# Recurrence of a chunked delta rule: the output values of all four chunks behind the last state, and the gram matrices in two groups of two chunks

## What is computed

```python
def step(S, inp):                      # reference, once per token
    r_t, w_t, k_t, v_t, a_t, b_t = inp
    sa = jnp.einsum('bhij,bhj->bhi', S, a_t)
    S = S * w_t[:, :, None, :] + sa[..., None] * b_t[:, :, None, :] + v_t[..., None] * k_t[:, :, None, :]
    y_t = jnp.einsum('bhij,bhj->bhi', S, r_t)
    return S, y_t
```

## Time and profile before

| | |
|---|---|
| median of 3 runs | 1474.78 us (1473.46 to 1477.78) |
| span of the profiled execution | 1471.8 us |
| PE, matmuls | 1432.0 us busy, 97% |
| DVE | 691.5 us busy, 47% |
| ACT | 514.4 us busy, 35% |
| POOL | 579.4 us busy, 39% |
| granted clock of PE | 9 tenths or more of full speed in all 40 slices |

### The profile page before, as it was taken

The page is one execution under the profiler, slowest core; times in us unless marked ns, Lnnn a source line. Parts: engine busy times, 40 slices in busy tenths (PEclk is TensorE's granted clock), DMA queues, the critical chain, the costliest instruction groups (busy, mean ns, idle before and its releaser), DMA issues.

```text
span 1471.8 us, 34271 instructions
## 1 busy us (share of the span) xinstructions
PE 1432.0 (97%) x14670; PEld 1344.3 (91%) x14670; DVE 691.5 (47%) x1447; ACT 514.4 (35%) x856; POOL 579.4 (39%) x740
## 2 busy tenths in 40 slices
PE   4999999999999999999999999999999999899998
PEld 4998999999999899999999999989999899699998
DVE  7117475664847557475664435343353444500000
ACT  6233242422514233242422544434444343322221
POOL 6353241422424134241422434434344443954442
PEclk9999999999999999999999999999999999999999
DMA  5333131311313113131311853735537375345361
GB/s 198 84 91 89 35 94 37 82 53 45 89 38 84 44 45 104 26 98 38 83 52 38 204 134 90 166 94 144 129 95 166 93 170 127 131 130 158 102 165 45
DMA packets 252084, 143.08 MB, mean 97 GB/s; under 512 B 12109, under 2 KB 245006, under 8 KB 251406
## 3 DMA queue, kind: packets, MB, share of 16 engines
q1 hardware_dynamic: 228316, 125.90, 33.6%
q10 hardware_dynamic: 23618, 15.00, 3.5%
HBM read 125.36 MB, written 15.45 MB: 96 GB/s over the span
## 4 chain that ended last, share of the span: by engine, by line
PE 85%; DVE 4%; POOL 3%; ACT 1%; issue 1%; ACTq 0%; DVEq 0%; POOLq 0%
PE acc L483 57%; PE head_banks L929 3%; PE head_banks L934 3%; PE head_banks L919 2%; PE head_banks L871 2%; PE head_banks L1077 1%; PE head_banks L1097 1%; POOL XL L764 1%; PE head_banks L997 1%; PE head_banks L1090 1%; PE head_banks L1046 1%; PE head_banks L986 1%; PE head_banks L838 1%; PE head_banks L967 1%; PE head_banks L886 1%
## 5 line engine op out<-in xcount | busy, mean ns | idle before, releaser
L466 POOL TENSOR_TENSOR WL<-WR,WH 128x256 fp32r<-128x256 f32 (+1 forms) x656 | 507.1, 804 | 858.9 <-ACT WH L456 838.5
L483 PE MATMUL acc<-XH,WH 128*128 128x260 f32 (+1 forms) x2624 | 569.4, 298 | 9.5 <-POOL WL L466 6.9
L483 PE MATMUL acc<-XH,WL 128*128 128x260 f32 (+1 forms) x2624 | 528.5, 283 | 0.0
L483 PE MATMUL acc<-XL,WH 128*128 128x260 f32 (+1 forms) x2624 | 527.7, 283 | 0.0
L483 PEld LDWEIGHTS acc<-XH,WH 128*128 128x128 f32 (+1 forms) x2624 | 404.6, 188 | 39.9 <-issue 28.7
L483 PEld LDWEIGHTS acc<-XL,WH 128*128 128x128 f32 (+1 forms) x2624 | 404.3, 188 | 0.0
L483 PEld LDWEIGHTS acc<-XH,WL 128*128 128x128 f32 (+1 forms) x2624 | 403.7, 188 | 0.0
L456 ACT ACTIVATE WH<-WR 128x1024 fp32r<-128x1024 f32 (+1 forms) x164 | 171.5, 1048 | 121.9 <-PE acc L483 114.6
L491 ACT ACTIVATE AREN<-acc 128x520 f32<-128x520 f32 (+1 forms) x82 | 49.4, 603 | 362.1 <-PE acc L483 354.8
L1929 DVE TENSOR_TENSOR AREN<-head_banks,AREN 128x512 f32<-128x512 f32 x16 | 11.1, 692 | 169.1 <-PE head_banks L1148 169.1
L1723 DVE TENSOR_TENSOR AREN<-AREN,head_banks 128x128 f32<-128x128 f32 x160 | 46.3, 289 | 33.3 <-PE head_banks L929 19.0
(11 more groups left out here) (238 smaller groups left out, 1597.5 us busy)
## 6 DMA issues: line engine op xcount, KB each, us to landing
WR<-in_w_in SPq DMA_DIRECT2D x128, 512.0 KB, 4.1
WR<-in_w_out SPq DMA_DIRECT2D x32, 512.0 KB, 6.9
out<-AREN ACTq DMA_DIRECT2D x32, 256.0 KB, 3.2
AREN<-in_cache_k_win SPq DMA_DIRECT2D x16, 384.0 KB, 8.0
AREN<-in_cache_v_win SPq DMA_DIRECT2D x16, 384.0 KB, 8.9
mix_scratch<-AREN ACTq DMA_DIRECT2D x16, 260.0 KB, 4.2
AREN<-in_x_prompt SPq DMA_DIRECT2D x4, 1024.0 KB, 7.6
AREN<-in_cache_k_win SPq DMA_DIRECT2D x8, 512.0 KB, 6.9
```

The costliest lines, as they stand in the source:

```text
L466: rest = pool.tensor_tensor(WL[:, place, j:j + 2, 0:M], WR[:, k % 4, j:j + 2, 0:M], WH[:, place, j:j + 2, 0:M].bitcast(F32), ALU.subtract)
L483: mm = pe.matmul(acc[0:M, hf, 0:HT], w[:, (4 * g + k) % 3, j, 0:M], x[:, kt, hf * HT:(hf + 1) * HT], start=(kt == 0 and n == 0), stop=(kt ...
```

## The change

The output values of all four chunks are computed in one run behind the last state (`values`), instead of each behind the `rhs` of the next chunk, and signal one step instead of four. In chunks 1 to 3 one projection unit follows `rhs`, and three instead of four follow `s` in chunks 0 to 2. Of the grams, chunks 0 and 1 stand in one group as before, now followed by 3 units; chunks 2 and 3 stand in one group behind `nn01`, with no unit in between and with other banks; `tokb`, `tokk`, `tokv` and `nn23` change their banks, and wait for the masks g20, g21, g30 and g31 in this order (before: `tokk` for g30, `tokv` for g31); 3 units instead of 4 follow `nn23`. The sum of units stays 64. ACT and POOL follow with their feeds: the rounding at unit 49 moves from behind `u2` to behind `rhs3`.

```diff
--- before.py
+++ after.py
@@ -161,12 +161,12 @@
 LV = range(1, LEVELS)
-GRAMS = ("g00", "g01", "g10", "g11", "g20", "g21", "nn01", "g30", "g31")
+GRAMS = ("g00", "g01", "g10", "g11", "nn01", "g20", "g21", "g30", "g31")
 UNITS = 4 * KT
-BEHIND_A = {"lora": 4, "kk": 3, "tail": 5, "bonus": 4, "vec": 4, "g11": 1, "g21": 1, "tokb": 2, "nn23": 4, "dx2b": 2, "dx4b": 2,
+BEHIND_A = {"lora": 4, "kk": 3, "tail": 5, "bonus": 4, "vec": 4, "g11": 3, "tokb": 2, "nn23": 3, "dx2b": 2, "dx4b": 2,
             "qt6b": 1, "dx6b": 1,
-            "rhs0": 1, **{f"u{c}": 1 for c in range(NC)}, **{f"s{c}": 4 for c in range(NC - 1)}, f"s{NC - 1}": 1,
-            f"y{NC - 1}": 2, "st": 2, "mean": 3}
+            **{f"rhs{c}": 1 for c in range(NC)}, **{f"u{c}": 1 for c in range(NC)}, **{f"s{c}": 3 for c in range(NC - 1)},
+            f"s{NC - 1}": 1, "values": 2, "st": 2, "mean": 3}
 QB = T // 128
 JS = [(h, b) for b in range(QB) for h in range(2)]
 BEHIND_B = {"ssum": 6, "tokv": 2, "stok": 2, "qb": 13,
@@ -383,8 +383,7 @@
                       *[x for l in LV if l < last
                         for x in (f"qt{l}a", f"qt{l}b", f"dy{l}a", f"dx{l}a", f"dy{l}b", f"dx{l}b")],
                       *[f"{s}{last}{h}" for s in ("qt", "dx") for h in "ab"],
-                      *[x for c in range(NC) for x in (f"rhs{c}", *([f"y{c - 1}"] if c else []), f"u{c}", f"s{c}")],
-                      f"y{NC - 1}", "st", "mean", "var"])
+                      *[f"{s}{c}" for c in range(NC) for s in ("rhs", "u", "s")], "values", "st", "mean", "var"])
         ACT_A = Steps(["ksq", "sgw", "sga", "sgg", "tail", "e1", "e2", "ln", "rn", "g", "dcs", "vec",
                        "nn01", "tokb", "tokk", "tokv", "nn23",
                        "fa", "q6b", "fb",
@@ -891,19 +890,19 @@
                 grams(0, (2, 3))
                 pe.wait_ge(a_act, ACT_A.at(i, "vec"))
                 grams(1, (0, 1))
-                pe.wait_ge(a_dve, DVE_A.at(i, "g01"))
-                grams(2, (2, 3))
                 pe.wait_ge(a_dve, DVE_A.at(i, "g11"))
                 transposed_n(0, 0, "nn01")
+                grams(2, (2, 3))
+                pe.wait_ge(a_act, ACT_A.at(i, "nn01"))
+                grams(3, (1, 0))
                 pe.wait_ge(a_dve, DVE_A.at(i, "g20"))
-                grams(3, (1, 2))
-                pe.wait_ge(a_act, ACT_A.at(i, "nn01"))
-                by_token("tokb", 0, BT)
+                by_token("tokb", 2, BT)
+                pe.wait_ge(a_dve, DVE_A.at(i, "g21"))
+                by_token("tokk", 3, KTL)
                 pe.wait_ge(a_dve, DVE_A.at(i, "g30"))
-                by_token("tokk", 1, KTL)
+                by_token("tokv", 1, M3[:, 2])
                 pe.wait_ge(a_dve, DVE_A.at(i, "g31"))
-                by_token("tokv", 2, M3[:, 2])
-                transposed_n(2, 3, "nn23")
+                transposed_n(2, 0, "nn23")
                 for l in range(1, last):
@@ -968,8 +967,7 @@
                                   skip_group_check=True)
                         mm = pe.matmul(out, U[:, c, cols], GR[:, c, 4 * h + 1, :], start=False, stop=True,
                                        skip_group_check=True)
-                    mm.then_inc(a_pe, PE_A.one(f"y{c}"))
-                    fill(f"y{c}")
+                    return mm
                 for c in range(NC):
                     if c == 0:
@@ -987,8 +985,6 @@
                                        stop=True, skip_group_check=True)
                     mm.then_inc(a_pe, PE_A.one(f"rhs{c}"))
                     fill(f"rhs{c}")
-                    if c:
-                        values(c - 1)
                     pe.wait_ge(a_act, ACT_A.at(i, f"rhs{c}"))
                     if c:
                         pe.wait_ge(a_act, ACT_A.at(i, f"u{c - 1}"))
@@ -1003,7 +999,10 @@
                     pe.matmul(HB[:, 2, 0:128], TOKB[:, c, :], U[:, c, :], start=False, stop=True)\
                         .then_inc(a_pe, PE_A.one(f"s{c}"))
                     fill(f"s{c}")
-                values(NC - 1)
+                for c in range(NC):
+                    mm = values(c)
+                mm.then_inc(a_pe, PE_A.one("values"))
+                fill("values")
                 pe.wait_ge(a_dve, DVE_A.at(i, f"s{NC - 1}"))
                 pe.transpose(HB[:, 3, 0:128], S[:, NC - 1, :], ident)
                 pe.matmul(HB[:, 3, 128:128 + NB], PXF[:, 0:128], ca["gather"], start=True, stop=True)\
@@ -1288,7 +1287,7 @@
                         act.activation(NN[:, 0:4, :].rearrange("p a b -> p (a b)"), HB[:, 0, :], ACT.Copy)\
                            .then_inc(a_act, ACT_A.one(name))
                     feed(name)
-                for name, bank, dst in (("tokb", 0, TOKB), ("tokk", 1, TOKK), ("tokv", 2, TOKV), ("nn23", 3, NN[:, 4:8, :])):
+                for name, bank, dst in (("tokb", 2, TOKB), ("tokk", 3, TOKK), ("tokv", 1, TOKV), ("nn23", 0, NN[:, 4:8, :])):
                     act.wait_ge(a_pe, PE_A.at(i, name))
                     act.activation(dst.rearrange("p a b -> p (a b)"), HB[:, bank, :], ACT.Copy)\
                        .then_inc(a_act, ACT_A.one(name))
@@ -1318,13 +1317,11 @@
                     act.wait_ge(a_pe, PE_A.at(i, f"rhs{c}"))
                     act.activation(RHS[:, c % 2, :], HB[:, 3, 0:128], ACT.Copy).then_inc(a_act, ACT_A.one(f"rhs{c}"))
                     feed(f"rhs{c}")
-                    if c:
-                        feed(f"y{c - 1}")
                     act.wait_ge(a_pe, PE_A.at(i, f"u{c}"))
                     act.activation(U[:, c, :], HB[:, 0, 0:128], ACT.Copy, scale=-1.0).then_inc(a_act, ACT_A.one(f"u{c}"))
                     feed(f"u{c}")
                     feed(f"s{c}")
-                feed(f"y{NC - 1}")
+                feed("values")
                 act.wait_ge(a_pe, PE_A.at(i, "st"))
                 act.wait_ge(o_state, done(0, i, 32))
                 act.activation(ST, HB[:, 3, 0:128], ACT.Copy).then_inc(a_act, ACT_A.one("st"))
@@ -1703,7 +1700,7 @@
                     after(f"xm{h}")
                     dve.tensor_tensor(xh, bc(ca["ident64"], 4), xh, ALU.subtract).then_inc(a_dve, DVE_A.one(f"x0{h}"))
-                for c, banks in enumerate(((2, 3), (0, 1), (2, 3), (1, 2))):
+                for c, banks in enumerate(((2, 3), (0, 1), (2, 3), (1, 0))):
                     if c == 3:
                         first_xt("a", 0)
                     for h in range(2):
```

## The result

The changed kernel takes 1488.78 us (median, 1488.34 to 1489.20), the kernel before 1476.23 beside it: ratio 1.0086, 95% interval 1.0071 to 1.0100. It is slower, by 12.6 us, where 5.6 was forecast; the time lies above the range. The profiled execution grew from 1471.8 to 1486.6 us, by 14.8. Two of the four runs of the kernel before took 1477.7 and 1477.8 us; beside the later experiments its medians are 1473.73, 1474.46 and 1475.37, so the loss lies between 12.6 and some 15 us. One of its 52 runs there took 2322.96 us at a mean granted clock of 0.553 and is not in the ratios.

The account below looks back on a forecast made before the run. PE's own list sets the time, with DVE as long in the gram stage; per pair -0.15 (recurrence) - 0.05 (grams) + 0.9 (DVE meeting POOL) = +0.7 us, eight pairs +5.6, so 1480.4 us; range 1471.5 to 1486.

Parts of the forecast that it names:

- The gram stage: Grams to level 1: PE's gain hidden by DVE's chain, -0.05 us a pair; DVE meeting POOL, +0.9 us.
- meeting: Before level 1, the second L1701 and L1704 on DVE each wait for a POOL subtraction, 0.9 us a pair.
- The term: Gram stage, per pair: -0.05 us from PE and DVE chains, +0.9 us from two DVE operations blocked by POOL.
- The price of one blocked operation: DVE operation with two SBUF inputs waiting for a POOL subtraction: between 0 and 0.7 us, taken as 0.45.
- rival 2: Before level 1, POOL first by a hair, all three DVE operations wait: +9.6 us, 1484.4; chance 0.14.
- The recurrence: Chunk steps rhs, u, state, values: 0.05 us saved times three, 0.15 us a pair, no new waits.
- the sum: Whole kernel: -0.15 - 0.05 + 0.9 = +0.7 us a pair, eight pairs +5.6 us on the span of 1471.8.
- The chance of slower, 0.53: Whole kernel: probability of a measurement slower by more than 0.3%, 4.4 us; within 0.35, faster 0.12.
- the most hopeful rival: Gram stage: DVE's chain is not last, PE keeps its gains, 0.55 us a pair, -4.4 us, 1470.4; chance 0.13.

Follow-up runs that it names:

- the one with the reductions ahead: Kernel before plus three unused DVE reductions ahead of `first_x("b")`, so that POOL's subtractions begin first: 1493.41 us against 1475.37, ratio 1.0107.
- the kernels with the state products first: Values behind the last state, products with the states before all half products: old gram stage 1467.56 us, changed kernel 1478.48, changed kernel with POOL held behind x0b 1468.66.
- grams alone: Changed kernel with the recurrence put back as before, so only the regrouped gram stage differs from the kernel before: 1484.66 us against 1473.73, ratio 1.0076.
- four reductions: Kernel before plus four unused DVE reductions between `first_x("b")` and the masks of level 1: 1493.28 us against 1474.46, ratio 1.0127.
- new run on the changed kernel: Changed kernel with the state products of all chunks first in the run of `values`: 1478.48 us against 1475.37 for the kernel before, ratio 1.0021.
- the kernel with units 2, 2, 4: Changed kernel with 2 units instead of 3 behind the grams of chunk 1 and 4 instead of 3 behind `nn23`: 1485.83 us against 1474.46, ratio 1.0074.
- two others: Changed kernel with POOL held behind x0b, 1477.37 us against 1473.73; the same with state products first in the run of values, 1468.66 against 1475.37.
- with three: Kernel before plus three unused DVE reductions between `first_x("b")` and the masks of level 1: 1476.39 us, ratio 1.0014.

## Why the prediction was right and where it was wrong

**The gram stage: right, and to size.** The chain of DVE, waits and meeting came as worked out: idle time ahead of chunk 2's masks 2.24 us (about 2.2 named), a short wait of `nn23` (315.24 - 314.17 = 1.07 instead of 0.87), L1701 at 0.83 (0.9 named), the waits for level 1 at 10.1 us (11 named), `dy1` at 14.59 (14.7). The term was +0.85 us a pair; measured 0.77. The price of one blocked operation, taken at 0.45 us from L1766, was 0.40 to 0.44. The order of the two engines, which decided between the forecast and rival 2, held by 0.06 us where 0.2 was named, so a part of this is luck. The Trainium skill (SBUF — State Buffer, "Who interferes with whom") calls the port that the two share an exclusive lock. The traces agree in direction: in the changed kernel and in the one with the reductions ahead, operations of DVE and of POOL are both longer (L1701 0.83 instead of 0.43 us, the four subtractions 3.35 instead of 2.92).

**The recurrence: wrong in sign.** -0.15 us a pair was forecast, +0.05 came. No new wait arose, as said: the states, ACT's copies and the rounding at unit 49 were all covered. The step that was mis-sized is "`values` alone cost 0.90, and perhaps 0.97 in a run": it was 1.02 a chunk. Behind a unit the half products started 0.31 us after the state product:

```profile
272.70 0.38 PE L961 MATMUL head_banks<-AREN 128*128 128x128 f32 x2
273.01 0.45 PE L967 MATMUL head_banks<-AREN 128*64 128x128 f32 x4
```

In the run, where the state product follows half products, it is 362.28 - 361.86 = 0.42. The 0.2 us between forecast and measurement weigh 1.6 us in all. The Trainium skill (TensorEngine Tiling (Array Packing), "Key Properties") says that changing the tiling mode drains TensorE. The runs show 0.15 to 0.17 us for it; but the change leaves the number of such changes in a pair at eight, and only the kernels with the state products first have fewer.

**The clock: missing.** The step that failed is the sum, 8 x 0.7 us added to a span, as if a wait cost only its own length: it put the granted clock at nothing without a reason. In the profiled execution some 6.9 of 14.8 us are matmuls at 1.2 GHz in the levels behind the longer wait. That the longer wait does it is shown: of 40 pairs in five kernels with 1.0 us or more of idle time before `dy1` (the changed one, grams alone, four reductions, three ahead, new run on the changed kernel) nine had a fall about 17 us behind the first gram (16.5 to 17.2), at least one in each kernel; of 56 pairs in the seven others, with 0.15 to 0.43 us, none. The Trainium skill (TensorE: Matmul & The Clock Gate, "What's actually happening") says the clock is set by how busy PE has been. The nine falls agree with that in direction; the six falls at the end of the levels, with no longer wait in their pairs, are not explained by it. The prediction had the longer wait (some 11 us of them in all) and did not ask what PE does in the microseconds around it: matmuls of 32 and 64 columns in quarters of the array, with no unit between. That these are the reason why a wait of 1.1 us among matmuls of 260 columns had no such effect is argued; no run changed them.

**The rivals.** None of them held this; the highest, +9.6, was a longer meeting. The chance of slower, 0.53, and the range, which ended at 1486, were both set without the clock.

**Open.** Why the clock fell at the end of the levels in four pairs of the kernel with units 2, 2, 4 and in one each of two others, where PE idles only 0.05 to 0.2 us more before `dy1` than in the kernel before, and why it falls in some pairs and not in others with the same rows. All six of these falls are in kernels with the regrouped grams (48 pairs), none in the six kernels with the old gram stage (48 pairs), so a part of the regrouping in them is not ruled out; no experiment separates it. Each kernel has one trace, and the falls differ from run to run: the kernel before, too, had runs of 1475.38 to 1482.13 us at mean clocks of 0.990 to 0.993, for which there is no trace. The runs show the places and the counts, no more.

## What to carry to other kernels

When an engine's idle time is taken away from one place and given to another, write down its chain from the new start, and look at which other engine starts at its end: here two engines met that had missed each other, since POOL started as DVE's last operation ran. A wait of a microsecond on a matrix engine that is otherwise full may cost more than its length; here it did among small matmuls and did not among large ones. Ask what the clock will do, and give the upper end of the range that much room. Operations that change the shape of the array are worth sorting by shape: three products moved ahead gained 6.9 us, more than the 4.4 that the most hopeful rival gave to the change.

## What was not expected of the hardware

- A wait of 1.01 to 1.12 us instead of 0.42 us before level 1 made TensorE's clock fall from 2.4 to 1.2 GHz for 6.8 or 10.2 us in one or two of eight pairs; with four reductions the kernel took 17 us more than with three, of which the waits are 5.
- Six changes fewer between `128*128` and `128*64` matmuls took 1.0 us off each pair, so one costs 0.15 to 0.17 us by estimate.
- DVE operations of 256 elements with both inputs in SBUF take 0.83 to 0.86 us instead of 0.42 when they start behind one of POOL's subtractions, and 0.43 when POOL starts behind them.
